# V sums of a prompt as one dense product with a gate matrix, and U dots of two tiles as products

## What is computed

```python
s1 = jnp.einsum('thc,nc->thn', q[:, :, 0], keys1)      # 8 heads, 128 keys
s2 = jnp.einsum('thc,nc->thn', q[:, :, 1], keys2)
t1, i1 = lax.top_k(s1, 16)
t2, i2 = lax.top_k(s2, 16)
# the 16 best of the 256 sums, each an expert i1 * 128 + i2
gate = jax.nn.softmax(top_s, axis=-1)
u_e = u_tab[idx]                                       # (tokens, 8, 16, 1024)
v_e = v_tab[idx]
act = jax.nn.gelu(jnp.einsum('td,thkd->thk', h, u_e))
return jnp.einsum('thk,thkd->td', gate * act, v_e)
```

## Time and profile before

| what | value |
|---|---|
| time, median of 3 runs | 2352.54 us (2350.27 to 2353.4) |
| span of the profiled execution, from first to last instruction | 2350.5 us |
| PE busy | 2000.8 us, 85%, 10334 records |
| PEld busy | 834.1 us, 35% |
| DVE busy | 1662.3 us, 71% |
| ACT busy | 297.1 us, 13% |
| POOL busy | 1282.2 us, 55% |
| read from HBM | 781.60 MB |
| written to HBM | 11.11 MB |
| mean DMA rate over the span | 337 GB/s |

### The profile page before, as it was taken

How to read it: one execution, slowest core, us unless ns; L and a number is a source line. 1 busy time by engine, 2 the same in 40 slices (tenths; PEclk the granted TensorE clock), 3 DMA queues, 4 the chain that set the end, 5 groups by cost and what they waited for, 6 DMA issues and landing times.

```text
span 2350.5 us, 30536 instructions
## 1 busy us (share of the span) xinstructions
PE 2000.8 (85%) x10334; PEld 834.1 (35%) x10334; DVE 1662.3 (71%) x3929; ACT 297.1 (13%) x643; POOL 1282.2 (55%) x1562
## 2 busy tenths in 40 slices
PE   5999999989889997988889779999777777777677
PEld 4444444543546676532233123333111111111111
DVE  2897798875655439866676787667788888777753
ACT  1112222232112112111000100101000000000000
POOL 1342233214443324666667666667677777777774
PEclk8999999989999998999999999999999999999999
DMA  9885777688778648999999999999999999999997
GB/s 335 269 267 187 223 232 223 189 305 311 257 235 258 234 154 303 388 408 405 402 405 406 401 376 403 403 404 407 398 400 409 407 397 408 403 402 409 401 409 291
DMA packets 264650, 794.62 MB, mean 338 GB/s; under 512 B 33328, under 2 KB 64788, under 8 KB 263992
## 3 DMA queue, kind: packets, MB, share of 16 engines
q0 software_dynamic: 191008, 680.63, 76.9%
q1 hardware_dynamic: 73504, 112.20, 13.8%
HBM read 781.60 MB, written 11.11 MB: 337 GB/s over the span
## 4 chain that ended last, share of the span: by engine, by line
PE 39%; DMA 29%; POOL 16%; issue 8%; DVE 5%; ACT 1%; PEld 0%; POOLq 0%; SPq 0%; PEldq 0%; DVEq 0%; ACTq 0%
DMA arena<-in_peer_v,arena 25%; POOL arena L1011 16%; PE banks L1036 13%; PE banks L1663 7%; PE banks L1331 3%; PE banks L1460 2%; PE banks L1193 2%; PE banks L1198 2%; DMA arena<-in_cache_v 2%; DMA arena<-in_w_ada 2%; DVE arena L2947 1%; PE banks L1042 1%; PE banks L1184 1%; PE banks L1185 1%; PE banks L1135 1%
## 5 line engine op out<-in xcount | busy, mean ns | idle before, releaser
L1663 PE MATMUL banks<-arena 128*32 128x512 f32 x2048 | 928.7, 604 | 246.7 <-DMA arena<-in_peer_v,arena 242.6
L2947 DVE CUSTOM_DVE_ANT_0 arena<-arena,banks 128x1024 f32<-128x1024 f32 x496 | 602.6, 1216 | 305.9 <-DMA arena<-in_peer_u,arena 302.4
L1011 POOL DMA_INDIRECT arena<-in_peer_v,arena x520 | 498.6, 959 | 264.0 <-PE banks L1663 132.6
L1011 POOL DMA_INDIRECT arena<-in_peer_u,arena x520 | 500.2, 962 | 201.4 <-issue 150.3
L1663 PEld LDWEIGHTS banks<-arena 128*32 128x32 f32 x2048 | 181.7, 110 | 910.9 <-DMA arena<-in_peer_v,arena 514.9
L1036 PE MATMUL banks<-arena 128*128 128x128 f32 (+6 forms) x1512 | 375.5, 403 | 9.6 <-DVE arena L2225 2.7
L987 POOL DMA_DIRECT2D arena<-in_cache_k x256 | 137.4, 537 | 323.1 <-DVE arena L2166 224.9
L1732 ACT ACTIVATE arena<-banks 128x512 f32<-128x512 f32 (+12 forms) x360 | 154.9, 430 | 1188.9 <-PE banks L1695 348.9
L1036 PEld LDWEIGHTS banks<-arena 128*128 128x128 f32 (+2 forms) x1512 | 233.2, 188 | 153.0 <-issue 134.7
L987 POOL DMA_DIRECT2D arena<-in_cache_v x256 | 137.4, 537 | 231.5 <-PE banks L1331 176.2
L2161 DVE TENSOR_TENSOR arena<-arena 128x512 f32<-128x512 f32 x256 | 175.5, 686 | 20.3 <-DMA arena<-scratch_queries 16.5
(11 more groups left out here) (304 smaller groups left out, 1627.6 us busy)
## 6 DMA issues: line engine op xcount, KB each, us to landing
arena<-in_cache_k POOLq DMA_DIRECT2D x256, 256.0 KB, 3.4
arena<-in_cache_v POOLq DMA_DIRECT2D x256, 256.0 KB, 4.5
arena<-in_w_ada SPq DMA_DIRECT2D x12, 2048.0 KB, 13.7
arena<-in_w_in SPq DMA_DIRECT2D x10, 2048.0 KB, 12.3
arena<-in_peer_wq SPq DMA_DIRECT2D x16, 1024.0 KB, 17.0
arena<-in_peer_u,arena POOLq DMA_INDIRECT x520, 10.7
arena<-in_peer_v,arena POOLq DMA_INDIRECT x520, 10.6
scratch_gates<-arena SPq DMA_DIRECT2D x16, 256.0 KB, 3.5
```

The costliest lines, as they stand in the source:

```text
L1011: nc.gpsimd.indirect_dma_start(gathered[:, j, :], None, tables[kind[0]][:, :], OFF(ap=index, axis=0)).then_inc(row_in[j], 16)
L1663: ins = mm(acc[u][32 * j:32 * (j + 1), :], spread[:, n % 2, b, :], gathered_row(("v", t, x))[:, 512 * u:512 * (u + 1)], start=x < 4, stop= ...
L2947: release(nc.vector.tensor_tensor_reduce(out=row, in0=row, in1=h2[:, t, :] if x < WIDE_AT else h2_wide, scale=1.0, scalar=0.0, op0=MUL, op ...
```

## The change

The loop of 536 slots becomes one of 290 (SLOTS_ALL) with U gathers for tiles 0 and 1 alone (256 slots), and a phase for V is added behind it.

- **U of tiles 2 and 3.** The whole table U is read once by SP, 128 blocks of 128 experts (0.52 MB each), from slot 65 on, two blocks in three slots. TensorE transposes a block (8 times 128 x 128) and multiplies it by the transposed tokens of both tiles (8 times `mm` of 128 x 256); ACT moves both results out of the banks, and stores four blocks of dots at a time to a scratch tensor in HBM (16.8 MB in all).
- **Gate matrix.** For each tile the indices and the gate of each slot are transposed (`turn_picks`). For each token POOL builds two matrices of slots by 128, one with ones at the first index, one with the gate at the second; TensorE multiplies them (`gate_products`, four tokens in a group, 32 groups a tile), ACT copies the group, and eight groups are stored (2 MB, runs of 1 KB). For tiles 0 and 1 the gate already holds the gelu; for tiles 2 and 3 it doesn't. For tile 3 VectorE builds the first of the two matrices.
- **V.** After a barrier, 16 blocks of 1024 experts: SP loads 2 MB of gates, 1 MB of dots and 4 MB of V for each, all laid out in whole rows. ACT and VectorE make the gelu of the dots and multiply the gates of tiles 2 and 3 by it. TensorE adds 64 `mm` of 128 x 512 to eight banks, two per tile. The weights of these are columns of `expert_gates`, eight numbers (32 bytes) apart.
- **Order.** The `rest` pieces move closer (MIX_AT 55 to 25, OUT_AT 102 to 42, ASK_AT 180 to 65). VectorE makes the choices of tile 2 and of the sample in the 16 heads of slots that are left, and those of tile 3 after them. The ring of rows has 8 places. The outputs of all tiles come at the end.

The core of the diff (first the constants, then POOL, TensorE, TensorE's V phase, and VectorE behind its loop of 16 heads):

```diff
-ROW_RING = 12
+ROW_RING = 8
+MIX_AT = 25
+OUT_AT = 42
+NORM_AT = 54
+ASK_AT = 65
+ASK_STEP = 4
+DENSE_AT = 65
+SLOTS_ALL = 290
+GATE_TILES = (0, 2, 1, 3)
+GATES_AT = (150, 200, 258)
+def dense_tiles(x):
+    return [i for i in range(KEYS) if DENSE_AT + 3 * i // 2 == x]
+def gate_groups(x):
+    for k, at in enumerate(GATES_AT):
+        for j in range(GROUPS_OF_TILE):
+            if at + (j if k == 2 else 3 * j // 2) == x:
+                yield k, j
...
+            def ones_of(k, j):
...
+                for r in range(FOUR):
...
+                    if k < 3:
+                        nc.gpsimd.tensor_scalar(first_ones[:, m % 2, r, :], steps, first, None, ALU.is_equal).then_inc(first_ready, 1)
+                    nc.gpsimd.tensor_scalar(second_ones[:, m % 2, r, :], steps, second, weight, ALU.is_equal, ALU.mult)\
+                        .then_inc(second_ready, 1)
+            for x in range(DOTS):
+                gather(x)
+                for k, j in gate_groups(x + 2):
+                    ones_of(k, j)
...
+            def turn_experts(i):
+
+                pe.wait_ge(u_in[i % U_RING], 16 * (i // U_RING + 1))
                 for u in range(2):
+                    o = begin(f"ut{i}_{u}")
+                    for k in range(4):
+                        ins = turn(o[:, P * k:P * (k + 1)], u_rows[:, i % U_RING, P * (4 * u + k):P * (4 * u + k + 1)])
+                    end(ins, f"ut{i}_{u}")
+            def expert_dots(i):
+                read(pe, f"ut{i}_1")
+                end(product_of(begin(f"a{i}")[:, 0:2 * P], [(u_t[:, i % 2, P * k:P * (k + 1)], h2_t[:, k, 0:2 * P])
+                                                            for k in range(KD)]), f"a{i}")
+            def gate_products(k, j):
+                m = GROUPS_OF_TILE * k + j
+                pe.wait_ge(first_ready, FOUR * (m + 1))
+                pe.wait_ge(second_ready, FOUR * (m + 1))
+                o = begin(gate_job(m))
+                for r in range(FOUR):
+                    ins = mm(o[:, P * r:P * (r + 1)], second_ones[:, m % 2, r, :], first_ones[:, m % 2, r, :], start=True, stop=True)
...
+            for b in range(EXPERT_BLOCKS):
+                for t in range(NT):
+                    if t == 0:
+                        pe.wait_ge(gates_in[b % 2], 16 * (b // 2 + 1))
+                    if t == 2:
+                        pe.wait_ge(gates_done, b + 1)
+                    for i in range(LANES):
...
+                        for u in range(2):
...
+                            ins = mm(bank(f"y{t}_{u}")[:, :], expert_gates[:, b % 2, P * t:P * (t + 1), i],
+                                     v_ring[:, pair % V_RING, D * half + 512 * u:D * half + 512 * (u + 1)], start=n == 0, stop=n == KEYS - 1)
...
+            run(choose(3, 0))
+            run(sample_columns())
+            for h in range(1, PH):
+                run(choose(3, h))
...
+            run(tile_gates(3))
+            for j in range(GROUPS_OF_TILE):
+                first_ones_of(j)
+            end_phase(dve, CHAIN + 1)
```

More of the change, by code:

```diff
@@ L28 @@
 RING = 8
-ROW_RING = 12
+ROW_RING = 8
+PAGE_TURNS = 2 * NS * PAGES // RING
 C = 64
@@ L56 @@
                   ("hsel", NC * 32), ("hspread", NC * P), ("center", P),
-                  ("part", BLOCK), ("half", BLOCK), ("block", TOP), ("place", TOP * 32), ("pick", TOP), ("owner", NS), ("owners", P)]:
+                  ("steps", P), ("pick", TOP), ("owner", NS), ("owners", P)]:
     CONST[_name] = (_at, _n)
@@ L62 @@
 CONST_C = CONST["gmask"][0]
-CONST_D = CONST["part"][0]
+CONST_D = CONST["steps"][0]
 PAR = {}
@@ L106, in constants @@
     put("fold", (p[:, None] % 32 == np.arange(H)[None, :]) * 1.0)
[L107 to L111, removed]
+    put("steps", np.broadcast_to(np.arange(P) * 1.0, (P, P)))
     put("pick", (p[:, None] % TOP == np.arange(TOP)[None, :]) * 1.0)
@@ L376, in psum_jobs @@
             fixed(u, f"{name}_{u}")
+    for t in range(NT):
+        for u in range(2):
+            fixed(2 * t + u, f"y{t}_{u}")
     place, used, r = {}, [0] * 8, 0
@@ new lines, in _ @@
+            v_of = peer_v.rearrange("l (a b) d -> b (l a) d", b=KEYS)
+            by_block = scratch_a.rearrange("p (n x) -> p n x", n=EXPERT_BLOCKS)
+            read(sp, "h2s")
+            for i in range(U_RING):
+                load(u_rows[:, i, :], u_of[:, i, :], u_in[i])
+            for x in range(DENSE_AT, SLOTS_ALL):
+                h, off = divmod(x - ASK_AT, ASK_STEP)
+                if off == 0 and 0 <= h < PH - 2:
+                    late_weights(f"wq1_{h + 2}")
+                for i in dense_tiles(x):
+                    if i + U_RING < KEYS:
+                        full(sp, f"ut{i}_1")
+                        load(u_rows[:, i % U_RING, :], u_of[:, i + U_RING, :], u_in[i % U_RING])
@@ L1011, in _ @@
                 nc.gpsimd.indirect_dma_start(gathered[:, j, :], None, tables[kind[0]][:, :],
-                                             OFF(ap=index, axis=0)).then_inc(row_in[j], 16)
+                                             OFF(ap=index, axis=0)).then_inc(slot_in[j], 16)
+            def ones_of(k, j):
+                m = GROUPS_OF_TILE * k + j
+                if j == 0:
+                    read(pool, f"picks{GATE_TILES[k]}")
+                if m >= 2:
+                    full(pool, gate_job(m - 2))
+                for r in range(FOUR):
+                    at = FOUR * j + r
+                    first, second, weight = (picks_t[:, k % 2, e, at:at + 1] for e in range(3))
+                    if k < 3:
[6 more added lines that the diff above has]
+                    ones_of(k, j)
+            for j in range(GROUPS_OF_TILE):
+                if j == 6:
+                    for h in range(PH):
+                        gather(DOTS + h)
+                if j == 18:
+                    for h in range(PH):
+                        gather(DOTS + PH + h)
+                ones_of(2, j)
+            for j in range(GROUPS_OF_TILE):
+                ones_of(3, j)
         @block.tensor
@@ L2074, in _ @@
             gate_exp(1)
-            for x in range(NT * SLOTS + LAG):
+            for x in range(SLOTS_ALL):
                 now[0] = x
@@ L2101, in _ @@
+            for t in range(NT):
+                root(t, P, NT + 3 + t)
         @block.vector
```

619 lines of the change are left out of this document (356 added, 263 removed).

## The result

| | before | changed |
|---|---|---|
| median | 2352.97 us (2350.27 to 2357.99, 4 runs) | 3177.59 us (3175.08 to 3181.93, 4 runs) |
| span of the profiled execution | 2350.5 us | 3174.5 us |
| read / written in HBM | 781.60 / 11.11 MB | 562.24 / 60.39 MB |

Ratio 1.3507, 95% interval 1.3476 to 1.3537: 35% slower. I had forecast 2909 us, 24% slower, in a range of 2820 to 3090. The direction was right and the time outside the range.

What follows compares the result with a forecast made beforehand. It took DMA as the old bound from 907 us and TensorE as mainly the new one: 908 + 189 + 705 + 192 + 885 + 12 = 2891, with 16 for clock and prices 2907, median 2909 us; range 2820 to 3090.

Steps and rivals of the forecast that it cites:

- POOL's price: Gate matrices: each 128x128 tensor_scalar on POOL takes 0.35 us, hidden under TensorE up to 0.44 us a piece.
- Rival (a): Gate matrices: POOL is the bound, at 0.6 us a piece the kernel takes 3085 us; chance 0.08.
- Slots 0 to 64: Slots before the dense U blocks: VectorE sets the pace, 189 us, by 20 either way in the range.
- Slots 65 to 255: Slots with dense U blocks and gate products: TensorE's records sum to 705 us, DMA and VectorE hidden.
- After slot 255: Stretch between the last slot and the V products: 192 us, including tile 1's matrix 109 and tile 3's 45.
- the handover: Before the V products: last 2 MB gate store lands and first 2 MB of gates load, 25 us.
- V phase: Dense V products behind the barrier: 2048 TensorE records of 0.432 us, 885 us, DMA and VectorE hidden.
- Rival (b): V products: weights 32 bytes apart slow TensorE; at 0.60 us a record the total is 3250; chance 0.05.
- End: From the last product to the end of the span: 12 us, as before.
- Rival (c): Dense products cost one record per `mm`, halving their time; total 2266 us, faster; chance 0.02.
- TensorE can't run ahead: Slots 65 to 255: TensorE cannot use the other engines' slack, because nothing later is ready; no size given.
- No cost: Slots with gates: POOL's wait for TensorE's product two groups earlier delays gathers and dots but adds no time.

Runs made afterwards that it cites:

- experiment 5: Changed kernel with POOL building a group's four matrices in one 128x512 instruction instead of four of 128x128, gates of three of four tokens left out; 2975.86 us.
- experiment 2: Changed kernel with the first matrices of tiles 0 and 2 built by VectorE instead of POOL, nothing left out; 3105.01 us.
- 8: Changed kernel with all first matrices on VectorE, and V, the gate matrix and the U dots of tiles 2 and 3 in bf16; 2364.52 us, ratio to before 1.0043.
- 9: Kernel of 8 with matrices of ones in bf16, four groups deep instead of two, and a fifth matrix of each group on VectorE; 2246.36 us.
- 3: Changed kernel with all first matrices, tile 1's included, built by VectorE, POOL keeping only second matrices; 3034.78 us, ratio to before 1.2911.
- experiment 4: Changed kernel with the dense U dots of tiles 2 and 3 summing only the first of eight slices of the hidden size; 3110.93 us.

## Why the prediction was wrong

**The step that failed** is POOL's price: "An eighth of the latter is 0.25, plus 0.1 for the start: 0.35, and I take that". Measured: 0.60 and 0.80, in the mean 0.70, which is beyond the 0.44 us at which, by the text's own reckoning, POOL passes TensorE. Both halves of the estimate were short: the column costs 2.6 and 3.4 ns instead of 2, the start 0.28 and 0.37 us instead of 0.1, and the nearest row to that 0.1 is the MEMSET of one column, 0.11 us, another instruction. I also took one price for two forms. By the 1.03 cycles an element of the Trainium skill (GPSIMD Engine Reference, section 3.1) the estimate was 0.21 us; the trace disagrees, with 0.60 for the form with one operation and 2.55 ns a column, an estimated 3 cycles at the same 1.2 GHz, and by the skill's figure the forecast would have been 33 us further off.

The text's own steps with the measured price: slots with gates 1.86 + 5.6 = 7.5 instead of 5.4 us, 64 times, +131; tile 1 256 x 0.70 + 20 = 199 instead of 109, +90; tile 3 128 x 0.79 = 101 instead of 45, +56. With the 2907 that is 3184, against a span of 3174.5. So this one price carries the miss; the 10 us that are left come of smaller terms, which partly cancel. Rival (a), which I gave 0.08, was the case; its own 3085 was 90 us low, because it stopped at 0.6 us.

Point by point:
- Slots 0 to 64: 189 forecast, 203 measured (910.7 to 1114.0 us). Off by 14, inside the 20.
- Slots 65 to 255: 705 forecast, 826 measured (1114.0 to 1940.4), 712 once POOL is relieved (experiment 5). The TensorE sum held once POOL was relieved, and was not the bound.
- After slot 255: 192 forecast, 342 measured; 203 of it tile 1, 102 tile 3, 21.7 the wait for the first V, where I had 25 for the handover.
- V phase: 885 forecast, 881 measured, with the forecast 2048 records. Rival (b), strided weights, is shown to cost nothing.
- End: 12 forecast, 11 measured. Rival (c): every float32 `mm` has two records; one record each came only with bf16.
- "TensorE can't run ahead" held. "No cost" for the wait two groups back held only because POOL was the slowest; once it wasn't, POOL waited for TensorE's gate products, 68 us in experiment 2 and 54 in 8.

**The range** ended at 3090; its own terms, 176 and 20 on 2909, give 3105, which would have missed too. It was that low because POOL's upper end was cut to 0.6 us, while the bound that I had named was the 2.0 us of a 1024-column instruction. A price without a row, on an engine a quarter away from its break point (0.35 against 0.44), deserved that whole side of the range and more than 0.08.

## What to carry to other kernels

A change that saves bytes leaves TensorE's records as they were; if they had been hidden under the transfers, they come out whole, and a barrier puts them end to end. Work that is built for TensorE by another engine is priced per instruction first (here 0.3 to 0.4 us before the first column) and compared with TensorE's pace in that very stretch, not with the engine's share of the span. When one engine of a ring is relieved, the depth of the buffers between them can be the next bound (argued here from the waits of experiments 2, 8 and 9, not shown by a run of its own).

## What the runs showed that I had not expected

- POOL's tensor_scalar on 128 columns of float32: 0.60 us with one operation, 0.80 with two; 1.58 and 2.11 us on 512 columns. Where VectorE builds matrices beside it, the form with two took 0.82 to 0.83 us in the mean (experiments 2, 3 and 8). VectorE does the one-operation form on 128 columns in 0.33 us (L3003, mean of 128, median 0.30).
- TensorE's clock was granted at 0.50 from 1960 to 2100 us, its lower level of 1.2 GHz, after 1690 to 1960, in which it was busy 213 of 270 us at 0.90; in the stretch itself it was busy 45 of 140. Eight gate records then took 2.05 us. It cost nothing there, since POOL took 5.43. With 400 us of its work removed (experiment 4) it was granted 0.67 in the gates.
- A weight load of 128 columns 32 bytes apart takes 314 ns, contiguous 190; beside a product of 430 ns both vanish.
